# One more expert position added back by matmul, and a modulation sum formed behind the norm

## The reference, cut to what matters

```python
mod_l = split((silu(c) @ ada_w[i] + ada_b[i]), 6)        # shift, scale, gate twice
h     = rmsnorm(x, norm_mix_g) * (1 + scale) + shift
x     = x + gate * mixer(h)                              # layer 0: attention + mLSTM, layer 1: 2-D DFT
f     = rmsnorm(x, norm_ffn_g) * (1 + scale') + shift'
y = 0
for e in range(16):
    he = silu(f @ w_gate[e]) * (f @ w_up[e])
    y  = y + combine[:, e:e+1] * (he @ w_down[e])
x = x + gate' * y                                        # and rmsnorm(x, final_g) after layer 1
```

## Time and profile before

| | |
|---|---|
| runs | 972.03, 973.26, 973.8 us |
| profiled execution, its own time | 973.74 us |
| span in the profile | 971.9 us |
| TensorE busy | 801.9 us (83%) |
| VectorE busy | 401.4 us (41%) |
| ScalarE / GpSimd busy | 178.0 us / 37.9 us |
| moved by DMA | 320.36 MB, mean 330 GB/s |
| chain that ended last | TensorE 38%, DMA 26%, VectorE 14%, SP's queue 12%, issue 5% |

### The profile page before, as it was taken

How to read it: one execution, slowest core, us unless ns; L and a number is a source line. 1 busy time by engine, 2 the same in 40 slices (tenths; PEclk the granted TensorE clock), 3 DMA queues, 4 the chain that set the end, 5 groups by cost and what they waited for, 6 DMA issues and landing times.

```text
span 971.9 us, 18143 instructions
## 1 busy us (share of the span) xinstructions
PE 801.9 (83%) x6954; PEld 432.2 (44%) x6955; DVE 401.4 (41%) x930; ACT 178.0 (18%) x383; POOL 37.9 (4%) x63
## 2 busy tenths in 40 slices
PE   8899989997979685978567986799869979697674
PEld 3544636444554343544234543374335535354332
DVE  3267879867878841211011230433621111112215
ACT  3222010326630111111001110240211110101002
POOL 0000000120000010000000000100010000000010
PEclk9799999999989797999777998799989988899798
DMA  9899977999505987959999999995669899999991
GB/s 342 292 371 348 335 268 269 330 361 314 197 2 216 379 311 277 366 201 414 415 417 415 371 375 413 372 410 227 247 253 412 349 415 415 416 414 416 414 369 56
DMA packets 102104, 320.36 MB, mean 330 GB/s; under 512 B 12704, under 2 KB 27424, under 8 KB 85536
## 3 DMA queue, kind: packets, MB, share of 16 engines
q1 hardware_dynamic: 78448, 282.84, 74.3%
q0 software_dynamic: 4592, 21.54, 5.9%
q10 hardware_dynamic: 19008, 15.22, 4.8%
HBM read 303.71 MB, written 24.25 MB: 337 GB/s over the span
## 4 chain that ended last, share of the span: by engine, by line
PE 38%; DMA 26%; DVE 14%; SPq 12%; issue 5%; ACT 3%; ACTq 2%; POOL 1%; DVEq 0%; POOLq 0%
DMA raw<-in_w_up 12%; DMA arena<-unit_rows 10%; PE bank L1809 8%; SPq L485 8%; PE bank L1588 7%; PE bank L1822 3%; PE bank L1969 3%; PE bank L1524 2%; DVE arena L929 2%; PE bank L1592 2%; PE bank L1597 1%; PE bank L1578 1%; DMA unit_rows<-arena,row_i 1%; SPq L454 1%; SPq L470 1%
## 5 line engine op out<-in xcount | busy, mean ns | idle before, releaser
L1809 PE MATMUL bank<-raw,arena 128*32 128x256 f32 x3392 | 245.7, 428 | 74.2 <-DMA raw<-in_w_up 41.5
L1809 PEld LDWEIGHTS bank<-raw,arena 128*32 128x32 f32 x3392 | 118.5, 120 | 181.1 <-DMA raw<-in_w_up 58.5
L1366 DVE TENSOR_TENSOR arena<-arena,bank 64x256 f32<-64x256 f32 x53 | 22.5, 425 | 339.0 <-ACT arena L814 339.0
L1822 PE MATMUL bank<-raw,arena 128*32 128x256 f32 x1696 | 111.6, 389 | 2.3 <-DVE arena L1354 2.3
L1822 PEld LDWEIGHTS bank<-raw,arena 128*32 128x32 f32 x1696 | 59.6, 113 | 41.4 <-issue 3.7
L1588 PE MATMUL bank<-ring,arena 128*128 128x512 f32 x160 | 69.9, 594 | 0.0
L814 ACT ACTIVATE arena<-bank 64x256 f32<-64x256 f32 x53 | 19.9, 376 | 246.9 <-PE bank L1809 225.5
L1796 PE MATMUL bank<-consts_sb,arena 64*128 64x64 f32 x212 | 36.1, 292 | 32.6 <-DVE arena L1366 21.2
L929 DVE SCALAR_TENSOR_TENSOR bias<-ring,small,bias 128x512 f32<-128x512 f32 x77 | 57.9, 752 | 2.7
L929 DVE SCALAR_TENSOR_TENSOR arena<-ring,small,arena 128x512 f32<-128x512 f32 x63 | 47.4, 752 | 2.2
L1796 PEld LDWEIGHTS bank<-consts_sb,arena 64*128 64x128 f32 x212 | 28.6, 194 | 44.1 <-DVE arena L1366 24.9
(11 more groups left out here) (259 smaller groups left out, 825.3 us busy)
## 6 DMA issues: line engine op xcount, KB each, us to landing
raw<-in_w_gate SPq DMA_DIRECT2D x64, 1024.0 KB, 19.8
raw<-in_w_up SPq DMA_DIRECT2D x64, 1024.0 KB, 21.7
raw<-in_w_down SPq DMA_DIRECT2D x64, 1024.0 KB, 22.7
ring<-in_ada_w SPq DMA_DIRECT2D x24, 2048.0 KB, 13.3
ring<-in_w_in SPq DMA_DIRECT2D x7, 2048.0 KB, 13.5
unit_results<-arena ACTq DMA_DIRECT2D x228, 32.0 KB, 7.2
arena<-unit_rows ACTq DMA_DIRECT2D x55, 128.0 KB, 6.9
ring<-in_w_out SPq DMA_DIRECT2D x2, 2048.0 KB, 42.8
```

The lines of the kernel that those rows point to most:

```text
L1809: ins = mm(ps[4][o:o + S, 0:FW], xT[:, i, j * S:(j + 1) * S], w[:, k % 4, h * FW:(h + 1) * FW], start=(k == 0), stop=(k == KD - 1))
L1822: ins = mm(ps[5][j * S:(j + 1) * S, 0:XW], hT_e[:, k % QN, k // QN * S:(k // QN + 1) * S], w[:, k % 2, j * XW:(j + 1) * XW], start=(k == 0 ...
```

## The change

There are four edits.

1. The seven small loads (gate columns, conv taps, router, biases, lambdas) leave SP's queue, where they stood behind the fifth ring load, and are issued by GpSimd once the third adaLN block has been used.
2. Block 22 takes the place `third` and block 23 goes to `bias[1]`. Block 23 is summed behind `mix_in(0)`, ahead of `route(0)`.
3. `ORDER[0]` changes: the second expert of layer 0 takes halves 8 to 13 and the third 6, 7 and 14 to 17, since half 6 and 7 lie where block 23's weights are. The wait on the saves covers only the even blocks.
4. Positions 14 and 15 (`LATE = NE - 2`) are both added by matmul. The fetch waits for the results of positions 0 to 13 only. `add_fetched` moves ahead of the product of position 15's first unit. Down comes before gate and up at position 14 too, and its results are scattered ahead of position 15's gate and up.

```diff
-        ORDER = [list(range(RAWS)),
+        ORDER = [list(range(NH)) + [8, 9, 10, 11, 12, 13, 6, 7, 14, 15, 16, 17],
...
-                    for b in range(2):
-                        sp.wait_ge(acc_saved[b], 16 * (N_ADA // 2))
+                    sp.wait_ge(acc_saved[0], 16 * (N_ADA // 2))
...
-                part = third if c == 2 * N_ADA - 1 else bias[:, c % 2, :]
+                part = third if c == 2 * N_ADA - 2 else bias[:, c % 2, :]
...
-                pool.wait_ge(L[l]["y_stored1"], (NE // 2 + 1) * 16 * JN)
+                pool.wait_ge(L[l]["y_stored1"], (NE // 2) * 16 * JN)
...
+            pool.wait_ge(w_used, 3)
+            pool.dma_start(wgt_s.rearrange("p (k n) -> p k n", k=KD),
+                           w_in_v[:, :, C_G:C_G + NE]).then_inc(smalls_in, 16)
...
-            for c in ADA_LATE:
+            for c in ADA_LATE[:-1]:
                 ada0(c)
...
+                for e in range(2):
+                    n_tok = dve.value_load(cnt_i[0:1, LATE + e:LATE + e + 1], min_val=0, max_val=SEQ)
+                    n = dve.snap(units, min_val=1, max_val=MAX_UNITS)
+                    turn_back(n - 1)
+                    if e == 0:
+                        result(n - 1, 0, NE // 2 - 1)
+                        dve.wait_ge(E["y_stored1"], (NE // 2) * 16 * JN)
+                    else:
                         late_result(n - 1)
+                        next_weights(1, True)
+                        add_fetched(l, 0)
+                        add_fetched(l, 1)
+                    product(n)
+                    turned(n + 1)
...
             mix_in(0, mod0[:, 0, :], mod0[:, 2, :], mod0[:, 1, :], mod0[:, 3, :], (gain_in, 32))
+            ada0(2 * N_ADA - 1)
             route(0)
...
+                for i in range(LATE, NE):
                     prev, own = own, held(i % HELD, i // HELD)
                     n_tok = pe.value_load(cnt_i[0:1, i:i + 1], min_val=0, max_val=SEQ)
+                    n = pe.snap(units, min_val=1, max_val=MAX_UNITS)
+                    turn_he(n - 1)
+                    down(n - 1, prev)
+                    if i > LATE:
                         scatter(n - 1, False)
+                    gate_up(n, own, True)
```

More of the change, by code:

```diff
@@ L951, in ada0 @@
                 else:
[L952 removed]
+                    ada_part(c, slot(s), third if c == 2 * N_ADA - 2 else bias[:, c % 2, :], wait_full
                              ).then_inc(acc_ready, 1)
@@ new lines, in next_weights @@
+                def next_weights(e, first):
+                    m = dve.snap(late, min_val=1, max_val=4 * UN)
+                    dve.wait_ge(scattered, m)
+                    if first:
+                        nc.vector.tensor_copy(late_at, cst("lane")).then_inc(late_ready, 1)
+                    else:
+                        nc.vector.tensor_scalar(late_at, late_at, float(S), None, ALU.add).then_inc(late_ready, 1)
+                    dve.wait_ge(late_ready, m * 2 + 1)
+                    late_weights(e)
+                    dve.reg_add(late, late, 1)
@@ L1884, in experts @@
                 own = held((NE - 4) % HELD, (NE - 4) // HELD)
-                for i in (NE - 3, NE - 2):
+                prev, own = own, held((LATE - 1) % HELD, (LATE - 1) // HELD)
+                n_tok = pe.value_load(cnt_i[0:1, LATE - 1:LATE], min_val=0, max_val=SEQ)
+                next_unit(prev, own, True)
+                pe.wait_ge(late_diag, l + 1)
+                for e in range(2):
+                    ins = mm(ps[2 + e][:], ones, bias[:, e, :], start=True, stop=True)
+                ins.then_inc(late_in_psum, 1)
@@ L1886, in experts @@
+                further(n_tok, own)
+                for i in range(LATE, NE):
                     prev, own = own, held(i % HELD, i // HELD)
                     n_tok = pe.value_load(cnt_i[0:1, i:i + 1], min_val=0, max_val=SEQ)
-                    next_unit(prev, own, True)
-                    if i == NE - 3:
-                        pe.wait_ge(late_diag, l + 1)
-                        mm(ps[2][:], ones, bias[:, 0, :], start=True, stop=True).then_inc(late_in_psum, 1)
-                    further(n_tok, own)
@@ new lines, in experts @@
+                    turn_he(n - 1)
+                    down(n - 1, prev)
+                    if i > LATE:
+                        scatter(n - 1, False)
+                    gate_up(n, own, True)
+                    turn_x(n + 1, True)
+                    pe.reg_add(units, units, 1)
+                    with pe.If(n_tok > S):
+                        with pe.Fori(S, n_tok, S):
+                            n = pe.snap(units, min_val=1, max_val=MAX_UNITS)
+                            turn_he(n - 1)
+                            gate_up(n, own, False)
+                            down(n - 1, own)
+                            turn_x(n + 1, False)
+                            scatter(n - 1, False)
+                            pe.reg_add(units, units, 1)
```

129 lines of the change are left out of this document (49 added, 80 removed).

## The result

The changed kernel took 980.7, 984.03, 985.24 and 987.79 us, median 984.63, against 973.53 for the kernel before beside it: ratio 1.0109, 95% interval 1.0065 to 1.0152. It is slower by about 1.1%, where 965.1 was forecast. The profiled execution is the shortest of the four, 980.7 us with a span of 978.9, so its rows show 7 us of loss against the earlier trace rows and not the 11 of the medians.

What follows compares the result with a forecast made beforehand. TensorE bounds the start, VectorE's chain 309 to 372 us, TensorE and short DMAs to about 425, the weight stream each layer's end. Terms -0.6 - 8.5 - 2.1 + 3.2 - 0.6 = -8.6 from 973.74: 965.1 us, range 960.5 to 971.0.

Steps and rivals of the forecast that it cites:

- Small loads: At the start: ring load out 13.2 us earlier, TensorE's 0.59 us wait gone; -0.6 us, bounds -0.6 and +1.
- The sums and the norm: Layer 0, mixer to scatter: route starts 6.6 us earlier, scatter's last piece gains another 1.9; -8.5 us, bounds -6.6 and -9.6.
- The lower bound of the term: Layer 0's route and scatter: least gain expected, -6.6 us, if the scatter itself gains nothing.
- The end of layer 0: Layer 0's tail: fetch delays the last up half 5.05 us, yet PSUM adds start at 625.9, not 627.98; -2.1 us.
- the first gain: The 8.5 us from the reordered sums, norm and scatter in layer 0, expected to carry through to the later stream.
- The end of layer 1: Layer 1's tail: fetch puts 5.05 us ahead of the last up half, tail adds save 1.85; +3.2 us.
- Left-out stores: Position 14's store, 128 KB a layer, left out: 0.3 us each in a full stream, -0.6 us.
- The late fetch: Both layers' ends: fetch waits behind queued weights, lands about 10 us later, adds delay the product; 985 us, chance 0.06.
- The cheap fetch: Both layers' ends: the fetch's 2.1 MB fit into holes and cost the stream little; 958.2 us, chance 0.10.
- The other two: Stream near layer 0's end takes the 8.5 us back, 973.6 us, chance 0.07; norm's gain not got, 968 us, within forecast's range.
- the norm's gain: Around layer 0's norm: might be missed through a late bias row or TensorE's slow clock; 2 to 3 us back, 968 us.
- wrong signs: Last up half in its old distance, product waiting for fetched rows well past its silu, or no stream hole at 400-420 us.

Runs made afterwards that it cites:

- Edit 1 alone: Only the seven small loads moved to GpSimd's queue, against the kernel before: 973.01 us, ratio 0.9987.
- The hold run: Changed kernel with fetched-row adds back behind the last unit, plus layer 0's third expert's six halves held until the scatter landed: 967.64 us, ratio 0.9919 to the kernel before.
- the adds at the tail: Changed kernel with the adds of the fetched rows back behind the last unit in both layers: 972.04 us, ratio 0.9969 to the kernel before.
- edits 1 to 3 together: Small loads on GpSimd, block 23 summed behind the norm and the ring order turned, without edit 4, against the kernel before: 974.20 us, ratio 0.9994.
- the run with the silu first: Changed kernel, fetched-row adds behind the last unit, each layer's first silu ahead of ScalarE's scatter wait: 967.62 us, ratio 0.9927 to the kernel before.
- the run with the adds early in layer 0 only: Changed kernel with fetched-row adds ahead of the product in layer 0, at the tail in layer 1: 978.15 us, ratio 1.0038 to the kernel before.

## Why the prediction was wrong

Two steps failed. The scatter's last piece was taken to land in 5.9 us and took 11.05, so of a gain of 8.5 us some 1.7 were left. And in each layer the fetch was taken to cost the last up half 5.05 us, and the adds of its rows, moved ahead of the product, next to nothing on top. It was the other way round: the up half lost 1.1 us in layer 0 and nothing in layer 1, and the adds of the late rows held up the product that TensorE waits for by 7 us and more. The terms one by one:

**Small loads, -0.6.** Edit 1 alone: -0.9 us, from -2.9 to +0.5. The wait of 0.59 us is gone. The stretch of the earlier trace rows has a lower clock instead, 0.82 to 0.89 in the eleven profiles with edit 1 against 0.87 to 0.95 in the three without (PE, PEld, DVE, ACT and POOL busy, clock, DMA share, GB/s from 42 to 60 us; before, then after):

```profile
42.00:60.00 18.00, 17.41 (x36) 7.52 (x37) 9.93 (x24) 5.56 (x14) 0.48 (x1) 0.90 0.91 339
```

```profile
42.00:60.00 18.00, 17.86 (x36) 8.00 (x37) 9.23 (x22) 4.78 (x13) 0.51 (x1) 0.85 1.04 387
```

**The sums and the norm, -8.5; measured -1.7.** VectorE's part was right: fourth residual 325.93 (forecast 325.3), router 339.51 (339.2). The step that failed is the scatter: "I take 5.9 us for the last piece". It took 11.05. The forecast had all eight halves through by 355.2 us and the scatter alone behind them. Packets, MB and share from 335.5 to 356.5 us show why they were not:

```profile
q1 hardware_dynamic: 1203, 6.64, 79.8%
q0 software_dynamic: 224, 0.79, 9.2%
q10 hardware_dynamic: 576, 0.39, 5.8%
```

The weights (q1) had no packet before 336.4, 1.5 us later than taken. Beside them went GpSimd's gain row (0.5 MB) and last save (0.26 MB), which had gone at 322 to 325 us and now go at 340, and 0.39 MB of ScalarE's stores: 1.9 and 1.0 us at 414 GB/s. The engines moved 389 GB/s and not 414, which is 1.8 us over all the bytes, the scatter's too. The forecast end of 360.5 plus these four is 366.7; the last packet came at 366.9 and the landing at 367.4. The forecast also overlooked the order of SP's queue. Halves 6 and 7, which wait for block 23's sum, stand ahead of 14 to 17, so six of the eight were issued behind the sum:

```profile
335.49 1.08 SPq L479 DMA_DIRECT2D raw<-in_w_down  x2
339.62 0.34 SPq L479 DMA_DIRECT2D raw<-in_w_gate  x1
```

That is 4.7 us later than taken, but it cost little: the two halves issued at 335.49 landed at 340.5 and 343.8 and kept the engines busy until the six came (1.38 MB of weights moved from 339 to 343 us). And a reading of the rows before was wrong. The 7.80 us of the earlier trace rows were not spent under six halves, since 0.25 MB of weights was all that moved beside the scatter's packets there. From first issue to last landing it was 3.0 us longer than in layer 1 (11.7 against 8.7), and its first packet came 3.1 us later behind the first issue (4.6 against 1.6). So little was to be won by having fewer halves left. TensorE's slow clock adds 1 us between router and scatter (15.8 us before, 16.8 after): behind 3.90 us of idle time ten matmuls of the route took 2.31 us, 1.19 before, and the windows from 344 to 352 us have the granted clock at 0.55 and 0.60.

```profile
344.00:348.00 4.00, 2.96 (x11) 2.63 (x12) 1.04 (x6) 0.00 (x0) 0.00 (x0) 0.55 1.01 416
348.00:352.00 4.00, 4.00 (x10) 1.42 (x12) 3.24 (x18) 0.00 (x0) 0.00 (x0) 0.60 1.03 421
```

The lower bound of the term, -6.6 "no gain on the scatter", was no bound: a transfer whose company grows can lose. The hold run confirms the cause as the traffic; how the scatter would go with the gain row and the save at their old place, no run shows.

**The end of layer 0, -2.1; measured about +3.** Release (forecast 597, measured 594.90), pair landed (607.8 and 611.9; 607.3 and 612.7) and product (614.5; 615.40) came nearly where they were put. But these times are counted ahead of the first gain: the stream was to be 8.5 us earlier still by then, and at position 15's first up half it was 3.4 (597.98 against 601.37). And "the last up half lands at ... 612.0", 5.05 us late for the fetch's sake, failed: it came at 604.70, and the two up halves stand 6.7 us apart where it was 5.6, so the fetch cost 1.1. Its packets began only 4.2 us behind its issue, 0.9 of its 2.1 MB went ahead of that half, and the rest shared with the down halves behind it. So the adds and not the weights were late, by 7 us; against the kernels without edit 4 (32.87 to 33.57 from p25 to a0) the tail is some 3 us longer.

**The end of layer 1, +3.2; measured +7.0 behind an upstream gain of 1.7 (at p49) to 3.1 (at the last up half), so +9 to +10.** The main step that failed is the same in both layers: the fetch's bytes were charged to the last up half, and of the adds the forecast said "they cost nothing on top". The up half lost nothing here and the product waited for the rows. One reason is "release 15.2 earlier, less 2", taken from the length of one expert and not from the rows. Against the upstream shift it came 8.4 us earlier (issued at 939.04 before; 939.04 - 3.07 - 927.55), since before, position 14's result stood only 3.7 us behind position 13's. The fetch was forecast 13 us ahead of the last up half and was 5.5 ahead. Its packets began 4.2 us behind the issue, 0.25 MB of them went ahead of that half, which kept its distance from the up half before it (5.5 us), and it landed 10.4 us behind it. From product to PSUM adds the forecast had 20.6 us and 23.2 were measured: the 2.5 us more are the slow clock behind the idle stretch (5.71 us for 64 matmuls against 3.66, 1.11 for four against 0.66), which the term left out.

**Left-out stores, -0.6.** Not measured alone; with the adds at the tail the whole of edit 4 is worth nothing that can be told.

By the measured sizes the sum is -0.9 - 1.7 + 3 + 9.5, about +10, against the forecast's -8.6 and the 11 us of the medians.

**The rivals.** The late fetch, given 0.06, named the place (the adds ahead of the product), the point of decision and the time, 985 against 984.63. Its mechanism was only half right. The fetch did not wait until the queued weights were through; its first packet came 4.2 us behind the issue, where it was 1.7 in layer 1 before, at the end of the stream. Then it shared the engines in halves, and the layer's last up half came before it instead of behind. The Trainium skill ("DMA: Bandwidth & Descriptors", "Queues, rings and completion order") has each DMA engine go round its queues packet by packet, and the queues' 0.43 and 0.39 MB in 2 us agree with it. The prediction drew on the same rule, but let the share begin at the issue and charged it to the up half. The cheap fetch, 0.10, was right on the weights (the last up half lost nothing in layer 1) and wrong on what that is worth, since VectorE's order tied the product to the rows all the same. Both rivals were one case: weights early, rows late. Their sum was priced in neither. The other two: most of the first gain was lost, but in the scatter and not in the stream near the end, and the norm's gain was got. Of what the forecast had named as wrong signs two came true: the last up half in its old distance, and a product that waits for the fetched rows well past its silu.

## What to carry to other kernels

An instruction that waits for a transfer belongs behind everything that the next engine waits for, until the transfer's landing has been shown to be earlier. When work is moved ahead, list what is queued behind each wait on the loading engine, and ask what the saved time lets run beside the next short transfer: here holding back 6 MB of weights for 20 us was worth 4.4 us, more than edits 1 to 3 together. And look for a wait that stands ahead of work that doesn't need it, as the silu behind the scatter did.

## What was not expected of the hardware

A 128 KB load of rows took 2.29 us when the stream stood still (368.21 to 370.50 in the run with the silu first) and 6 to 8.3 beside it. GpSimd's indirect transfers, scatter and fetch alike, had their first packet 4.1 to 4.6 us behind their first issue beside a full stream, in all 14 profiles but for one fetch with 3.5; where the stream had paused or was ending it came after 1.6 to 1.7. What makes the difference no run shows. Beside running weights the transfer then had half of the engines.

TensorE's clock differs between executions of the same code at the same place. From 260 to 280 us it was granted 1.00 in the changed kernel and in twelve of the other profiles; in the run with the adds early in layer 0 only, whose program is the same up to there, 0.68:

```profile
260.00:280.00 20.00, 18.65 (x65) 11.60 (x65) 17.30 (x49) 7.75 (x20) 0.00 (x0) 0.68 0.00 1
```

That run's router starts at 343.83 us and not at 338.2 to 340.6 as in the six others with block 23's sum at that place and no hold. What made the clock fall there is open; it shows one way in which single profiles come to differ by 3 us or more. Whether the changed kernel's own profile, the shortest of its four, understated the loss for this reason isn't shown.
